# Splitting the next weights ahead of the normed input in the output products of a two-layer decoder step

## The chip, the cores and the metric

The kernel runs on one core of a Trainium2 chip. The metric is the device time of one execution, in microseconds (us). TensorE multiplies, VectorE and ScalarE work on tiles, GpSimd adds up squares, and SyncE issues the loads of the weights; each runs its own list of instructions in order, and they meet at semaphores. In the rows of the profile they are called PE (with PEld for its weight loads), DVE, ACT, POOL and SP.

## The reference

The reference is one inference step of a small decoder: 512 new prompt tokens and 8 sequences of 8 sample tokens, 576 tokens in all, of 1024 features. There are two layers. Each adds to the residual x a half SwiGLU, a mixer (gated delta rule in the first layer, stick-breaking attention in the second), another half SwiGLU, and a gated per-layer embedding. A projection that several of these end with has this form:

```python
x = x + 0.5 * _swiglu(_rms_norm(x, w['ffn1_norm'][i]), w['ffn1_w_in'][i], w['ffn1_w_out'][i])
h = _rms_norm(x, w['mix_norm'][i])
...
def _rms_norm(x, g):
    xf = x.astype(jnp.float32)
    y = xf * lax.rsqrt(jnp.mean(xf * xf, axis=-1, keepdims=True) + EPS)
    return (y * g.astype(jnp.float32)).astype(x.dtype)

def _swiglu(h, w_in, w_out):
    gu = h @ w_in
    gate, up = gu[..., :D_FF], gu[..., D_FF:]
    return (jax.nn.silu(gate) * up) @ w_out
```

All matrices are float32, D_FF is 2816.

## The kernel before

**Layout and arithmetic.** Activations lie transposed: features on the 128 partitions, 576 tokens in the free dimension. A product is computed tile by tile, each tile being 128 output features by 576 tokens. float32 values are kept as a high and a low part in TensorE's faster float32 format: for each block of 128 input features the function `multiply` (line 529) issues three matmuls, high by high, high by low and low by high, for each of two parts of the tokens. The parts are `PARTS = ((0, C0), (C0, T))` with `C0 = 288` and `T = 576`, so 288 columns each (lines 55 and 222). A tile with k blocks is thus 6k matmuls of 288 columns.

**Units and buffers.** Two tiles, m = 0 and m = 1, make a unit. The weights of a unit are loaded as one slot of `raw`, of which there are two. The split parts `w_hi` and `w_lo` have one place for m = 0 and one for m = 1. ScalarE makes `w_hi` with `split_hi` (line 478) as a rounded copy; it waits until the load has landed and until TensorE has finished the tile that last used that place. VectorE makes `w_lo` with `split_lo` (line 495) as the difference of `raw` and `w_hi`. So while TensorE works on one tile, the weights of the tile after it are split. SyncE loads a unit (`load_unit`, line 510) once `w_lo` of the unit two before it has been made.

**Output products.** A step of kind `upd` adds a product to the residual `xT`: four units, eight tiles, in the plan at lines 361 to 421. There are fourteen: three for each of the four SwiGLUs, over 8, 8 and 6 blocks of the hidden features (`GROUPS`, line 76), and one behind each mixer, over 8 blocks. Only the last of the three (6 blocks) and the two behind the mixers make the input of what follows. They carry `after` and `sums`: for each finished tile VectorE updates `xT` (line 3076), ScalarE makes `hx_hi`, the rounded x times gain, and `sqb`, the square (`act_renorm`, lines 2544 to 2554), VectorE makes `hx_lo` (`dve_renorm`, line 2564), and GpSimd adds the square to `ssum` (line 2581). The normalising factor is applied later, to the results of the next product: at that product's first tile TensorE sums `ssum` over the partitions (line 603) ahead of the last block, ScalarE takes the root into `std` (line 610), and VectorE the reciprocal into `rs` (line 614).

**What sets the order.** Everything is written out by hand. `in_pairs` (line 452) runs a body for each unit and tells it which tile's weights to split (`split`): those of the next unit of the step, and behind the last unit those of the first unit of the next step. In the six `upd` steps that carry `after`, the engines' bodies (lines 2929 to 2934 and 3071 to 3078) run, for each tile, first what the finished tile needs and then the split. In the other kinds of step, the `gu` step of the SwiGLU's input product for one, ScalarE splits first.

Of the kernel before, what the change touches and what calls it, by code (L numbers as in the profile page):

```python
# [48 lines left out]
def program(nc, A, O):  # L49
# [33 lines left out]
    with ctx:  # L83
# [160 lines left out]
        def halves(ap):  # L244
            return ap.rearrange("p (c n) -> p c n", c=2)

        def seqs(ap, n=TD):

            return ap.rearrange("p (b t) -> p b t", t=n)
# [85 lines left out]
        def pin_view(par, m):  # L335
            return praw[:, par].rearrange("p (k n) -> p k n", n=2 * P)[:, :, m * P:(m + 1) * P]
# [135 lines left out]
        def unit_no(s, i, r):  # L472
            return i * 2 + (s.n["unit"] + r)

        def slot_of(s, r):
            return raw[:, (s.n["unit"] + r) % 2, :], raw_in[(s.n["unit"] + r) % 2]

        def split_hi(act, target, m):

            s, i, r = target  # L480
            if s is None:
                return
            slot, landed = slot_of(s, r)
            k = (s.ka, s.kb)[m]
            act.wait_ge(landed, i * 32 + 32 * ((s.n["unit"] + r) // 2 + 1))
            if not (isinstance(i, int) and unit_no(s, i, r) == 0):
                act.wait_ge(tile_done, unit_no(s, i, r) * 2 + (m - 1))
            nc.scalar.activation(w_hi[:, m, 0:k], s.view(m, slot), ACT.Copy).then_inc(w_hi_done, 1)  # L488
            if s.kind == "ple":
                n = KD * s.n["ple"] + 2 * r  # L490
                if not (isinstance(i, int) and n + 4 * i + m < 2):
                    act.wait_ge(pin_done, i * 4 + (n + m - 1))
                nc.scalar.activation(pw_hi[:, m], pin_view((s.n["unit"] + r) % 2, m), ACT.Copy).then_inc(pw_hi_done, 1)
# [2047 lines left out]
        def x_rows_of(i):  # L2541
            return P if i < PT else TS

        def act_renorm(act, s, j, m):

            if s.after is not None:
                hi, hi_done = (hid_hi, hid_hi_done) if s.into is HID else (hx_hi, hx_hi_done)
                nc.scalar.activation(hi[:, ds(j, 1)], xT[:, ds(j, 1)], ACT.Copy,  # L2548
                                     scale=gain[:, ds(j + s.after, 1)]).then_inc(hi_done, 1)
            if s.sums:  # L2550
                q = KD * s.n["sum"]
                if not (isinstance(j, int) and q + j < 2):
                    act.wait_ge(ssum_done, j + (q - 1))
                nc.scalar.activation(sqb[:, m:m + 1], xT[:, ds(j, 1)], ACT.Square).then_inc(sq_done, 1)  # L2554

        def dve_renorm(dve, s, j):

            if s.after is not None:
                hi, lo = s.into or HX
                if s.into is HID:  # L2560
                    dve.wait_ge(hid_hi_done, j + (s.n["hid"] + 1))
                else:
                    dve.wait_ge(hx_hi_done, j + (KD * s.n["hx"] + 1))
                nc.vector.scalar_tensor_tensor(lo[:, ds(j, 1)], xT[:, ds(j, 1)], gain[:, ds(j + s.after, 1)],  # L2564
                                               hi[:, ds(j, 1)].bitcast(F32), ALU.mult, ALU.subtract
                                               ).then_inc(hid_done if s.into is HID else hx_done, 1)
# [330 lines left out]
        def _(act):  # L2897
# [6 lines left out]
            for s in plan:  # L2904
                def body(i, r, split):
                    N = unit_no(s, i, r)
                    u = i * 2 + r
                    first = isinstance(u, int) and u == 0 and s.stats and s.n["stat"]
                    if first:
                        act_stats(act, s.n["stat"])  # L2910
                    if s.kind == "gu":
                        split_hi(act, split, 0)
                        act.wait_ge(evac[0], N + 1)
                        if not (isinstance(u, int) and s.n["gu"] + u == 0):
                            act.wait_ge(hid_mul, u + s.n["gu"])
                        nc.scalar.activation(gate_f[:], gate_s[:], ACT.Silu).then_inc(silu_done, 1)
                        split_hi(act, split, 1)
                        act.wait_ge(hid_mul, u + (s.n["gu"] + 1))
                        nc.scalar.activation(hid_hi[:, ds(u, 1)], hid_f[:], ACT.Copy).then_inc(hid_hi_done, 1)  # L2919
                        move_rows(act, s, 1, fills_at(s, u, 1))  # L2920
                    elif s.kind == "lin":
                        if s.after is not None and u == 0:
                            act.wait_ge(tile_done, 2 * s.n["unit"])
                        for m in range(2):
                            if s.after is not None:
                                act_renorm(act, s, u * 2 + m, m)
                            split_hi(act, split, m)
                            move_rows(act, s, 1, fills_at(s, u, m))
                    elif s.kind == "upd":
                        for m in range(2):  # L2930
                            if s.after is not None or s.sums:
                                act.wait_ge(evac[m], N + 1 - m * (s.n["unit"] - s.n["eb"]))
                                act_renorm(act, s, u * 2 + m, m)
                            split_hi(act, split, m)
                    elif s.kind == "qkv":
                        for m in range(2):
                            c = u * 2 + m
                            split_hi(act, split, m)
                            act.wait_ge(evac[m], N + 1)
                            nc.scalar.activation(cv[:, m, 0:XC], xpad[:, m, 0:XC], ACT.Copy,  # L2940
                                                 scale=conv_w[:, 0, ds(c, 1)]).then_inc(tap_done, 1)
                            act.wait_ge(conv_step, c * CP + CP)
                            out = qkv[:, ds(c, 1)].squeeze(1)
                            nc.scalar.activation(out[:, 0:TP], cv[:, m, 0:TP], ACT.Silu).then_inc(conv_done, 1)
                            nc.scalar.activation(seqs(out[:, TP:T]), seqs(cv[:, m, CP + TP:], CP + TD)[:, :, 0:TD], ACT.Silu).then_inc(conv_done, 1)
                    elif s.kind == "ab":
                        ab_act(act, s, N, split)
                    elif s.kind == "gate":
                        for m in range(2 - s.alone):
                            gate_act(act, s, N, u, m, split)  # L2950
                    elif s.kind == "ple":
                        for m in range(2):
                            if s.end and (u, m) in ((2, 1), (3, 0)):
                                y_left(act, 2 * (2 * u + m - 5) + 1)
                            split_hi(act, split, m)
                            act.wait_ge(evac[m], N + 1 - m * (s.n["unit"] - s.n["eb"]))
                            buf = (gate_s, up_s)[m]
                            nc.scalar.activation(buf[:], buf[:], ACT.Sigmoid).then_inc(silu_done, 1)
                            act.wait_ge(x_add, u * 2 + (KD * s.n["ple"] + m + 1))
                            act_renorm(act, s, u * 2 + m, m)  # L2960
                            if s.end:
                                j = u * 2 + m
                                nc.scalar.activation(yT[:, j], xT[:, j], ACT.Copy, scale=gain[:, FIN + j:FIN + j + 1]).then_inc(y_done, 1)
                    else:
                        split_hi(act, split, 0)
                        split_hi(act, split, 1)
# [70 lines left out]
        def _(dve):  # L3037
# [4 lines left out]
            for s in plan:  # L3042
                def body(i, r, split):
                    N = unit_no(s, i, r)
                    u = i * 2 + r
# [25 lines left out]
                    elif s.kind == "upd":  # L3071
                        for m in range(2):
                            j = u * 2 + m
                            dve.wait_ge(tile_done, (tile_a, tile_b)[m])
                            x = xT[:, ds(j, 1)].squeeze(1)
                            nc.vector.scalar_tensor_tensor(halves(x), TOKENS[m], s.coef, halves(x), ALU.mult, ALU.add).then_inc(evac[m], 1)  # L3076
                            dve_renorm(dve, s, j)
                            split_lo(dve, split, m)
                    elif s.kind == "qkv":
                        for m in range(2):  # L3080
                            c = u * 2 + m
# [247 lines left out]
```

## Time and profile before

| what | value |
|---|---|
| median of 3 runs (lowest to highest) | 2609.31 us (2607.67 to 2610.5) |
| profiled execution, own time | 2611.66 us |
| its span | 2609.5 us |
| PE busy | 2547.4 us, 98% of the span |
| DVE, ACT, POOL busy | 51%, 35%, 10% |
| loads | 86 GB/s over the span |

The page of the profile gives each engine's busy time, the chain of work that ended last, and groups of instructions. The timeline lists instructions by start time with their durations and, in brackets, how long the engine had been idle before and what released it. Matmuls are pipelined: a matmul of 288 columns is shown with 0.29 us, but the next one starts some 0.12 us later, so TensorE's pace is read from start to start.

### The profile page before, as it was taken

Reading aid. Unit: us, or ns where it says so; the run is one execution under the profiler, and the core shown is the slowest. Engines: PE = TensorE matmul, PEld = TensorE weight load, DVE = VectorE, ACT = ScalarE, POOL = GpSimd, SP = SyncE. Lnnn points to the kernel's source line nnn. Section 1 sums busy time; section 2 is a strip of 40 time slices with the busy share of each in tenths; the row PEclk is TensorE's granted clock in tenths of the full one; section 3 lists DMA queues with packets and bytes.
Section 4 is the critical chain, followed back from the end, with each engine's and each line's share of the span. In section 5 each row is a group of like instructions: output and inputs, shape, how many; then the busy total and the mean of one; then the engine's idle time right before and its main releaser. Section 6 shows DMA issues by size and latency. Waiting matters only on the chain.

```text
span 2609.5 us, 52241 instructions
## 1 busy us (share of the span) xinstructions
PE 2547.4 (98%) x21981; PEld 2454.2 (94%) x21981; DVE 1325.9 (51%) x1739; ACT 916.6 (35%) x1384; POOL 270.4 (10%) x348
## 2 busy tenths in 40 slices
PE   8999999999999999999999999999999999999998
PEld 7999999998888999999999999999986699999998
DVE  4434347765555554343565443434557754344454
ACT  4222224454323432222343232222348832222244
POOL 2000002001223200000120000000133210000011
PEclk9999999999999899999999999999999999999999
DMA  5233322321011332332222442323303423232321
GB/s 149 81 87 90 93 72 93 97 81 32 20 36 52 99 97 88 89 96 81 85 93 81 126 135 81 96 81 89 116 14 106 146 81 90 88 93 85 93 97 57
DMA packets 308138, 225.96 MB, mean 87 GB/s; under 512 B 8270, under 2 KB 301567, under 8 KB 307967
## 3 DMA queue, kind: packets, MB, share of 16 engines
q1 hardware_dynamic: 307280, 224.26, 28.5%
q8 instruction: 82, 1.34, 0.2%
q14 instruction: 38, 0.31, 0.0%
q0 software_dynamic: 576, 0.00, 0.0%
q10 hardware_dynamic: 162, 0.04, 0.0%
HBM read 212.14 MB, written 12.13 MB: 86 GB/s over the span
## 4 chain that ended last, share of the span: by engine, by line
PE 92%; DVE 4%; ACT 2%; issue 1%; DMA 0%; POOL 0%; SPq 0%; DVEq 0%; POOLq 0%; ACTq 0%
PE ps L551 77%; DVE w_lo L503 1%; PE ps L2425 1%; PE ps L2459 1%; PE ps L570 1%; PE ps L1824 1%; PE ps L2467 1%; PE ps L1828 1%; PE ps L2364 1%; PE ps L1572 0%; ACT w_hi L488 0%; DVE xT L3076 0%; PE ps L2609 0%; PE ps L1835 0%; ACT sqb L2554 0%
## 5 line engine op out<-in xcount | busy, mean ns | idle before, releaser
L551 PE MATMUL ps<-hx_hi,w_hi 128*128 128x288 f32 x3730 | 1071.0, 287 | 4.0 <-DVE w_lo L503 3.2
L551 PE MATMUL ps<-hx_lo,w_hi 128*128 128x288 f32 x3730 | 1066.8, 286 | 0.0
L551 PE MATMUL ps<-hx_hi,w_lo 128*128 128x288 f32 x3730 | 1066.8, 286 | 0.0
L488 ACT ACTIVATE w_hi<-raw 128x1024 fp32r<-128x1024 f32 (+1 forms) x362 | 373.9, 1033 | 1095.7 <-PE ps L551 1095.3
L551 PEld LDWEIGHTS ps<-hx_hi,w_hi 128*128 128x128 f32 x3730 | 704.9, 189 | 8.0 <-DVE w_lo L503 4.0
L551 PEld LDWEIGHTS ps<-hx_lo,w_hi 128*128 128x128 f32 x3730 | 705.0, 189 | 0.3
L551 PEld LDWEIGHTS ps<-hx_hi,w_lo 128*128 128x128 f32 x3730 | 705.0, 189 | 0.0
L551 PE MATMUL ps<-hid_hi,w_hi 128*128 128x288 f32 x1920 | 554.0, 289 | 5.6 <-DVE w_lo L503 4.8
L551 PE MATMUL ps<-hid_hi,w_lo 128*128 128x288 f32 x1920 | 551.1, 287 | 0.0
L551 PE MATMUL ps<-hid_lo,w_hi 128*128 128x288 f32 x1920 | 551.0, 287 | 0.0
L503 DVE TENSOR_TENSOR w_lo<-raw,w_hi 128x1024 fp32r<-128x1024 f32 (+1 forms) x362 | 460.4, 1272 | 124.0 <-ACT w_hi L488 123.9
L551 PEld LDWEIGHTS ps<-hid_hi,w_hi 128*128 128x128 f32 x1920 | 364.6, 190 | 9.1 <-issue 8.6
L551 PEld LDWEIGHTS ps<-hid_hi,w_lo 128*128 128x128 f32 x1920 | 364.7, 190 | 0.1
L551 PEld LDWEIGHTS ps<-hid_lo,w_hi 128*128 128x128 f32 x1920 | 364.6, 190 | 0.0
L2581 POOL TENSOR_TENSOR ssum<-ssum,sqb 128x576 f32<-128x576 f32 x64 | 92.4, 1443 | 1808.1 <-issue 1216.5
L3060 DVE TENSOR_TENSOR up_s<-ps,rs 128x576 f32<-128x576 f32 x88 | 66.6, 757 | 308.0 <-PE ps L551 307.8
L3076 DVE SCALAR_TENSOR_TENSOR xT<-ps,xT 128x576 f32<-128x576 f32 x112 | 84.6, 755 | 249.8 <-PE ps L551 249.8
L3057 DVE TENSOR_TENSOR gate_s<-ps,rs 128x576 f32<-128x576 f32 x88 | 66.6, 757 | 215.4 <-PE ps L551 215.1
L2548 ACT ACTIVATE hx_hi<-xT,gain 128x576 fp32r<-128x576 f32 x56 | 43.3, 774 | 147.8 <-DVE xT L3076 147.8
L2919 ACT ACTIVATE hid_hi<-hid_f 128x576 f32 (+1 forms) x88 | 60.2, 685 | 54.9 <-DVE hid_f L3065 54.9
L2564 DVE SCALAR_TENSOR_TENSOR hx_lo<-xT,gain,hx_hi 128x576 fp32r<-128x576 f32 x64 | 51.9, 816 | 40.5 <-ACT hx_hi L2548 40.5
L3065 DVE TENSOR_TENSOR hid_f<-gate_f,up_s 128x576 f32<-128x576 f32 x88 | 66.7, 758 | 10.7 <-DVE up_s L3060 9.3
(477 smaller groups left out, 2277.9 us busy)
## 6 DMA issues: line engine op xcount, KB each, us to landing
raw<-in_ffn_w_in SPq DMA_DIRECT2D x176, 512.0 KB, 4.9
raw<-in_ffn_w_out SPq DMA_DIRECT2D x64, 512.0 KB, 4.0
raw<-in_a_w_in SPq DMA_DIRECT2D x33, 512.0 KB, 4.3
raw<-in_ffn_w_out SPq DMA_DIRECT2D x32, 384.0 KB, 3.4
raw<-in_ple_w_gate SPq DMA_DIRECT2D x8, 1024.0 KB, 5.2
raw<-in_w_kv SPq DMA_DIRECT2D x16, 512.0 KB, 4.1
k_page<-in_cache_k SPq DMA_DIRECT2D x16, 512.0 KB, 3.5
v_page<-in_cache_v SPq DMA_DIRECT2D x14, 512.0 KB, 4.8
```

The costliest lines, as they stand in the source:

```text
L488: nc.scalar.activation(w_hi[:, m, 0:k], s.view(m, slot), ACT.Copy).then_inc(w_hi_done, 1)
L503: nc.vector.tensor_tensor(w_lo[:, m, 0:k], s.view(m, slot), w_hi[:, m, 0:k].bitcast(F32), ALU.subtract).then_inc(w_lo_done, 1)
L551: last = nc.tensor.matmul(TILE[m][:, c0:c1], w[:, m, k], columns(h, k, c0, c1), start=k == 0 and a == 0, stop=k == k_all - 1 and a == 2)
L570: last = nc.tensor.matmul(PIN[:, c0:c1], w[:, m, k], columns(h, k, c0, c1), start=k == 0 and a == 0, stop=k == PK - 1 and a == 2)
L2548: nc.scalar.activation(hi[:, ds(j, 1)], xT[:, ds(j, 1)], ACT.Copy, scale=gain[:, ds(j + s.after, 1)]).then_inc(hi_done, 1)
L2564: nc.vector.scalar_tensor_tensor(lo[:, ds(j, 1)], xT[:, ds(j, 1)], gain[:, ds(j + s.after, 1)], hi[:, ds(j, 1)].bitcast(F32), ALU.mult, AL ...
L2581: nc.gpsimd.tensor_tensor(ssum[:], ssum[:], sqb[:, m], ALU.add).then_inc(ssum_done, 1)
L2919: nc.scalar.activation(hid_hi[:, ds(u, 1)], hid_f[:], ACT.Copy).then_inc(hid_hi_done, 1)
L3057: nc.vector.tensor_tensor(halves(gate_s[:]), TOKENS[0], halves(rs[:]), ALU.mult).then_inc(evac[0], 1)
L3060: nc.vector.tensor_tensor(halves(up_s[:]), TOKENS[1], halves(rs[:]), ALU.mult).then_inc(evac[1], 1)
L3065: nc.vector.tensor_tensor(hid_f[:], gate_f[:], up_s[:], ALU.mult).then_inc(hid_mul, 1)
L3076: nc.vector.scalar_tensor_tensor(halves(x), TOKENS[m], s.coef, halves(x), ALU.mult, ALU.add).then_inc(evac[m], 1)
```

## The change

A small test `at_end` is added, true for the last tile of a step. In `upd` steps the split of the next weights moves ahead, for each tile but the last: on ScalarE ahead of the wait for VectorE's update of `xT`, of `hx_hi` and of `sqb`; on VectorE to between the update of `xT` and `hx_lo`. For the last tile the order stays. The change's title also names equal parts of 288 columns; these are in the kernel before already and no line of the diff touches them.

```diff
+        def at_end(s, u, m):
+            return isinstance(u, int) and 2 * u + m == 2 * s.units - 1
+
...
                     elif s.kind == "upd":
                         for m in range(2):
+                            if not at_end(s, u, m):
+                                split_hi(act, split, m)
                             if s.after is not None or s.sums:
                                 act.wait_ge(evac[m], N + 1 - m * (s.n["unit"] - s.n["eb"]))
                                 act_renorm(act, s, u * 2 + m, m)
-                            split_hi(act, split, m)
+                            if at_end(s, u, m):
+                                split_hi(act, split, m)
...
                             nc.vector.scalar_tensor_tensor(halves(x), TOKENS[m], s.coef, halves(x), ALU.mult, ALU.add).then_inc(evac[m], 1)
+                            if not at_end(s, u, m):
+                                split_lo(dve, split, m)
                             dve_renorm(dve, s, j)
-                            split_lo(dve, split, m)
+                            if at_end(s, u, m):
+                                split_lo(dve, split, m)
```

The order of ScalarE's instructions at the end of the first SwiGLU's last output product, from its seventh tile on, before. `w_hi` of 128x1024 is a weight tile of the next step:

```order
L2548 ACTIVATE hx_hi<-xT,gain 128x576
L2554 ACTIVATE sqb<-xT 128x576
L488 ACTIVATE w_hi<-raw 128x1024
L2548 ACTIVATE hx_hi<-xT,gain 128x576
L2554 ACTIVATE sqb<-xT 128x576
L488 ACTIVATE w_hi<-raw 128x1024
L610 ACT_TABLE_LOAD
```

The same place with the change (the line numbers are three higher):

```order
L488 ACTIVATE w_hi<-raw 128x1024
L2551 ACTIVATE hx_hi<-xT,gain 128x576
L2557 ACTIVATE sqb<-xT 128x576
L2551 ACTIVATE hx_hi<-xT,gain 128x576
L2557 ACTIVATE sqb<-xT 128x576
L488 ACTIVATE w_hi<-raw 128x1024
L610 ACT_TABLE_LOAD
```

The seventh tile's split has moved ahead of its `hx_hi` and `sqb`; the last tile's stands where it stood.

VectorE at the same place, from the seventh tile's update of `xT` to the reciprocal, before:

```order
L3076 SCALAR_TENSOR_TENSOR xT<-ps,xT 128x576
L2564 SCALAR_TENSOR_TENSOR hx_lo<-xT,gain,hx_hi 128x576
L503 TENSOR_TENSOR w_lo<-raw,w_hi 128x1024
L3076 SCALAR_TENSOR_TENSOR xT<-ps,xT 128x576
L2564 SCALAR_TENSOR_TENSOR hx_lo<-xT,gain,hx_hi 128x576
L503 TENSOR_TENSOR w_lo<-raw,w_hi 128x1024
L614 RECIPROCAL rs<-std 128x576
```

And with the change:

```order
L3082 SCALAR_TENSOR_TENSOR xT<-ps,xT 128x576
L503 TENSOR_TENSOR w_lo<-raw,w_hi 128x1024
L2567 SCALAR_TENSOR_TENSOR hx_lo<-xT,gain,hx_hi 128x576
L3082 SCALAR_TENSOR_TENSOR xT<-ps,xT 128x576
L2567 SCALAR_TENSOR_TENSOR hx_lo<-xT,gain,hx_hi 128x576
L503 TENSOR_TENSOR w_lo<-raw,w_hi 128x1024
L614 RECIPROCAL rs<-std 128x576
```

`w_lo` and `hx_lo` have changed places for the seventh tile, as for the six before it, and not for the last. The lists of TensorE, GpSimd and SyncE are the same in both programs.

## Rows read from the trace of the kernel before

**Rows 1.** Page, part 1: busy us, share of the span, instructions.
```profile
PE 2547.4 (98%) x21981; PEld 2454.2 (94%) x21981; DVE 1325.9 (51%) x1739; ACT 916.6 (35%) x1384; POOL 270.4 (10%) x348
```

**Rows 2.** Waits of PE: waiting line, releaser, us in total, times, longest.
```profile
PE ps L551 <- DVE w_lo L503: 8.1, 21, 0.7
```

**Rows 3.** Chain that ended last: start us, us, what, of an undisturbed stretch.
```profile
932.33 345.70 PE ps L551 x2820
```

**Rows 4.** Timeline of PE, first, second and fourth SwiGLU's last output product: start us, us.
```profile
377.71 0.29 PE L551 MATMUL ps<-hid_hi,w_hi 128*128 128x288 f32 x1
...
401.02 0.29 PE L551 MATMUL ps<-hid_hi,w_hi 128*128 128x288 f32 x1
...
405.31 0.29 PE L551 MATMUL ps<-hid_lo,w_hi 128*128 128x288 f32 x1
...
405.97 0.36 PE L551 MATMUL ps<-hid_hi,w_hi 128*128 128x288 f32 x1 [0.38 <-DVE w_lo L503]
...
415.49 0.39 PE L551 MATMUL ps<-hx_hi,w_hi 128*128 128x288 f32 x1 [0.46 <-DVE w_lo L503]
...
1273.44 0.29 PE L551 MATMUL ps<-hid_hi,w_hi 128*128 128x288 f32 x1
...
1311.26 0.39 PE L551 MATMUL ps<-hx_hi,w_hi 128*128 128x288 f32 x1 [0.47 <-DVE w_lo L503]
...
2494.23 0.29 PE L551 MATMUL ps<-hid_hi,w_hi 128*128 128x288 f32 x1
...
2532.05 0.39 PE L551 MATMUL ps<-hx_hi,w_hi 128*128 128x288 f32 x1 [0.48 <-DVE w_lo L503]
```

**Rows 5.** Timeline of all engines around one tile, the first of the third unit.
```profile
401.22 0.76 DVE L3076 SCALAR_TENSOR_TENSOR xT<-ps,xT 128x576 f32<-128x576 f32 x1 [0.51 <-PE ps L551]
...
402.01 0.78 ACT L2548 ACTIVATE hx_hi<-xT,gain 128x576 fp32r<-128x576 f32 x1 [2.94 <-DVE xT L3076]
...
402.69 0.67 ACT L2554 ACTIVATE sqb<-xT 128x576 f32<-128x576 f32 x1
...
402.82 0.82 DVE L2564 SCALAR_TENSOR_TENSOR hx_lo<-xT,gain,hx_hi 128x576 fp32r<-128x576 f32 x1 [0.84 <-ACT hx_hi L2548]
...
403.27 0.83 ACT L488 ACTIVATE w_hi<-raw 128x768 fp32r<-128x768 f32 x1
...
403.44 1.48 POOL L2581 TENSOR_TENSOR ssum<-ssum,sqb 128x576 f32<-128x576 f32 x1 [3.55 <-ACT sqb L2554]
...
404.13 1.60 DVE L503 TENSOR_TENSOR w_lo<-raw,w_hi 128x768 fp32r<-128x768 f32 x1 [0.49 <-ACT w_hi L488]
```

**Rows 6.** Timeline of all engines, a tile of the input product before.
```profile
372.03 0.76 DVE L3057 TENSOR_TENSOR gate_s<-ps,rs 128x576 f32<-128x576 f32 x1 [2.53 <-PE ps L551]
...
372.09 0.84 ACT L488 ACTIVATE w_hi<-raw 128x768 fp32r<-128x768 f32 x1 [3.67 <-PE ps L551]
...
372.97 0.96 DVE L503 TENSOR_TENSOR w_lo<-raw,w_hi 128x768 fp32r<-128x768 f32 x1 [0.18 <-ACT w_hi L488]
```

**Rows 7.** Timelines of DVE, POOL and PE, last tile and start of the next product.
```profile
415.36 0.74 DVE L3076 SCALAR_TENSOR_TENSOR xT<-ps,xT 128x576 f32<-128x576 f32 x1
...
418.47 1.66 DVE L503 TENSOR_TENSOR w_lo<-raw,w_hi 128x1024 fp32r<-128x1024 f32 x1 [0.70 <-ACT w_hi L488]
...
417.56 1.48 POOL L2581 TENSOR_TENSOR ssum<-ssum,sqb 128x576 f32<-128x576 f32 x1 [3.21 <-ACT sqb L2554]
...
420.74 1.13 PE L603 MATMUL ps<-ssum,ones 128*128 128x288 f32 x4
```

**Rows 8.** Timeline of SP: issues of the third and fourth unit's weights.
```profile
380.36 11.84 SPq L516 DMA_DIRECT2D raw<-in_ffn_w_out  x4
```

**Rows 9.** Page, part 6: DMA issues, KB each, median us to landing.
```profile
raw<-in_ffn_w_out SPq DMA_DIRECT2D x32, 384.0 KB, 3.4
```

**Rows 10.** Timeline of DVE, one tile of the product behind the first mixer.
```profile
907.70 0.76 DVE L3076 SCALAR_TENSOR_TENSOR xT<-ps,xT 128x576 f32<-128x576 f32 x1 [1.08 <-PE ps L551]
...
910.83 1.66 DVE L503 TENSOR_TENSOR w_lo<-raw,w_hi 128x1024 fp32r<-128x1024 f32 x1 [0.70 <-ACT w_hi L488]
```

## The prediction

> **What bounds the kernel now.** I read the page first. TensorE is busy for 98% of the span [rows 1], and nearly all of the chain that ended last is its own matmuls, so a change of order on ScalarE and VectorE can only act where TensorE stands still for them. The table of TensorE's waits, read next, has one row on the split weights: 8.1 us in 21 waits, the longest 0.7 us [rows 2]. To see where these are I went through TensorE's timeline. Sixteen of the 21 lie in four places, four in each: the last output product (6 blocks) of each SwiGLU, at the start of its second, third and fourth unit and at the start of the product behind it. The rows show the third and fourth wait of the first place, at 405.97 and 415.49, and the last one of the second and of the fourth place [rows 4]. The two products behind the mixers have none in their inside.
>
> An idle time in brackets counts from a modelled end, so I measure the loss from start to start. Undisturbed, 2820 matmuls take 345.70 us [rows 3], 0.1226 us each. A unit here is 72 matmuls, 8.83 us; from 405.97 to 415.49 it took 9.52 us. At 405.97 the pieces are seen: the last matmul of the tile before started at 405.31, the next could have followed at 405.43 and came 0.54 us later, and a first matmul behind a wait takes a little under 0.1 us more. For the whole product, the four starts run from 377.71 to 415.49, 37.78 us; 37.82 us in the second and in the fourth place [rows 4]; the third, which repeats the pattern, has 37.80 us. Together 151.22 us. Without waits, 4 x 288 matmuls at 0.1226 us are 141.23 us. **The loss is 9.99 us.**
>
> Why TensorE waits there is read around one tile [rows 5]. TensorE starts the next tile at 401.02 [rows 4]; VectorE begins the update of x at 401.22, which I call E. ScalarE waits for the update, makes hx_hi and sqb, and starts w_hi only at 403.27, E+2.05. VectorE's w_lo starts at 404.13 and ends at 405.73, E+4.51. The tile that TensorE has meanwhile is worth 36 x 0.1226 = 4.41 us from 401.02, so it would need the weights at 405.43, E+4.21. They are late by 0.3 us, plus about 0.24 us from w_lo's end to the first matmul. After such a late start the next weights, counted from a delayed tile, come in time; hence one wait for each two tiles.
>
> **The change, part by part.** Nothing is added or removed. On ScalarE, w_hi (0.83 us) goes ahead of the wait for the update and of hx_hi (0.78) and sqb (0.67). It then needs only TensorE's tile and the landed load. The input product just before has this order, and there w_hi starts 0.06 us behind the evacuation, and w_lo 0.94 us behind it, to last 0.96 us [rows 6]. I take this as it stands for the new order: w_hi from E+0.06 to E+0.90, w_lo from E+0.94 to E+1.90. It is needed at E+4.21, so 2.3 us of slack takes the place of 0.3 us of lateness. For the weights of the next step, of 8 blocks, w_lo without company takes 1.22 us and w_hi 1.04, so E+2.36: still 1.85 us of slack. Both bounds of the gain follow: all of the loss, 9.99 us, if nothing else is late; nothing, if w_hi waits for something else. The rows of the input product are the nearest, so I take the upper end: **-10.0 us**.
>
> What is moved back: hx_hi would start at about E+0.8 (as before), sqb end at E+2.2 instead of E+2.14, and hx_lo run from about E+1.8 to E+2.6 instead of E+1.60 to E+2.42. These matter only at the next product, whose blocks are used in turn, 6 matmuls or 0.74 us each. The seventh tile's is used some 9 us after its tile ended, so 0.2 us are hidden. The last tile keeps its order. GpSimd's add starts at about E+2.3 instead of E+2.22 and must be done before the next one, 4.4 us later: hidden too.
>
> Loads: SyncE's waits hang on w_lo of every second tile, which now comes some 2.6 us earlier, so loads start earlier and none starts later. The other side is that w_hi now asks for its load up to 2 us earlier. The third unit's was issued at 380.36 [rows 8]; two pieces of 3.4 us one behind the other [rows 9] have landed by 387.2, while the tile after which it is asked for ends near 391.8. Slack 4.6 us: cost 0.
>
> Products behind the mixers: there w_lo ends at 912.49, 4.79 us behind E = 907.70 [rows 10], and a tile of 48 matmuls lasts 5.88 us. Nothing waits, so the new order is worth nothing there, 0. The other eight output products carry no input for what follows and are the same program on ScalarE, and on VectorE too. The equal parts of 288 columns are in both programs: 0.
>
> One thing more stands in these rows. w_lo of 128x768 takes 0.96 us where GpSimd rests [rows 6] and 1.60 us behind the add that runs from 403.44 to 404.92 [rows 5]; it ends 0.81 us behind the add's end. That is nearly all of its own time, as if it had stood still until then. Without these 0.64 us the weights would have been there at E+3.87 and TensorE would not have waited. In the new order w_lo is over before the add begins at E+2.3. The Trainium skill, "SBUF — State Buffer", section "Who interferes with whom", says that a VectorE instruction with two SBUF inputs contends with a GpSimd instruction that reads SBUF and that whichever came first holds the pair for its whole length. By that rule the trace agrees in both its numbers, and hx_lo, which would now come first, holds the add back by some 0.4 us, to end near E+4.1; by a mere sharing both would be a little longer. By the one the sum is 10.0 us and by the other too, but under the rule the company moves to hx_lo and the add and cannot follow w_lo.
>
> **What is late next.** At the start of the next product TensorE needs the sum of squares ahead of the last block. Now the last tile's update starts at 415.36, the add ends at 419.04, 3.68 us later, and TensorE comes to it at 420.74 [rows 7]. With the wait gone the product starts 0.20 us ahead of E, and 42 matmuls on, at E+4.95, it wants the sum; the add ends at E+3.68. So 1.3 us of slack remain, where there were 1.7. The second tile's weights are at 420.13, E+4.77 [rows 7]; they are needed after a whole tile and the sum's matmuls, about E+6.5. Neither turns into a wait.
>
> **The sum.** Profiled execution: 2611.66 - 9.99 = 2601.7 us, its span 2609.5 - 9.99 = 2599.5 us. That execution stands 2.35 us above the median of the runs, so for the median 2609.31 - 9.99 = **2599.3 us**, 0.38% faster. The three runs lie 2.8 us apart, and I call differences under 0.2%, 5.2 us, no change: from 2604.1 to 2614.5 us.
>
> **The rivals.** (A) The forecast. All sixteen waits go. Chance 0.84.
>
> (B) The twelve waits inside go, but the four ahead of the following product come back at its start, since that start hangs on the last tile's chain (update, sqb, add) and not on TensorE. Price: each is worth 9.52 - 8.83 = 0.69 us, so 2.8 us are given back: 2602.1 us. For it: the chain is unchanged for the last tile, and the slack shrinks. Against: 1.3 us are left. Chance 0.07.
>
> (C) The change does not do what it says: w_hi goes ahead in the list but waits, for the load or for TensorE's end of tile. All waits stay: 2609.3 us; half of them: 2604.3 us. For it: the new wait is for two semaphores, one of them the load. Against: the slack of 4.6 us and the input product, where just this order works. Chance 0.06, a third of it for half.
>
> (D) Slower. The sum of squares becomes the bound: split and lock together push sqb and the add of the last two tiles back until TensorE stands at the sum's matmuls at the six products that follow. It decides from 1.3 us of extra delay on. To lose 5.2 us against before it would have to eat 10 us of gain as well, 15.2 / 6 = 2.5 us each, so 3.8 us of delay. One w_hi and one w_lo with the add's stop are 0.83 + 1.60 = 2.4 us, and the last tile's order has neither ahead of it. Price at a full 4.4 us of delay (one tile): 6 x 3.1 = 18.6, less 10: 2618 us. Chance 0.03.
>
> **How the numbers follow.** Faster by over 0.2%: A, B and a little of C, 0.92. Within: the rest of C, 0.05. Slower: D, 0.03. The range takes A with the scatter of medians of about 2.5 us to either side, and on the upper side B and its scatter: 2596.8 to 2603.6 us. Half of C, C and D lie outside.
>
> **What would show it.** The waits of TensorE on w_lo fall from 21 to about 5 and from 8.1 us to about 1; each of the four products takes 35.3 us from its first matmul to that of the next; w_lo of 128x768 has about 0.96 us everywhere and starts 0.9 us behind the update of x; hx_lo or the add is the one that grows. The first matmul of the sum at the next product starts 5.15 us behind the product's first. I am wrong if waits on w_lo stay (C), if one on ssum or hx_lo appears at the next product (B, D), or if the stretch shrinks and a later one grows.

## The result and the profile after

The changed kernel takes 2596.69 us (median of 6 runs, 2592.87 to 2599.85), beside 2610.2 us of the kernel before (6 runs, 2607.67 to 2611.51). The ratio is 0.995, with a 95% interval from 0.9938 to 0.9962: 13 us faster, between 10 and 16. The forecast was 2599.3 us, 10.0 us faster, and the median lies 0.1 us below the low end of the range. The profiled execution took 2598.09 us, its span is 2596.0 us.

In TensorE's table of waits the row that it was all about has shrunk; what [rows 2] had as 8.1 us in 21 waits is now (total, times, longest):

```profile
PE ps L551 <- DVE w_lo L503: 2.5, 6, 1.5
```

All sixteen of the four places are gone. Of the 2.5 us left, 1.5 are a single wait at 18.5, right behind the kernel's start, which took 0.7 us before; the other five are 0.2 to 0.3 us each.

In the timeline of PE, the first of the four places. The columns are start and duration, in us:

```profile
377.64 0.29 PE L551 MATMUL ps<-hid_hi,w_hi 128*128 128x288 f32 x1
...
412.79 0.29 PE L551 MATMUL ps<-hid_lo,w_hi 128*128 128x288 f32 x1
...
412.92 0.29 PE L551 MATMUL ps<-hx_hi,w_hi 128*128 128x288 f32 x1
...
418.06 1.13 PE L603 MATMUL ps<-ssum,ones 128*128 128x288 f32 x4
```

From the output product's first matmul at 377.64 to that of the next product at 412.92 are 35.28 us, where [rows 4] had 37.78 (377.71 to 415.49). The last matmul before stands 0.13 us ahead of it: no wait is left. The chain that ended last says the same of a longer stretch. Before, it was broken at the second place's four waits; now TensorE's matmuls are in one piece from the second unit of the first product behind the first mixer to the start of the gated embedding, and in another, as long, behind the second mixer:

```profile
927.70 381.70 PE ps L551 x3114
...
2142.22 381.70 PE ps L551 x3114
```

381.70 / 3114 is 0.1226 us for each, the undisturbed pace of [rows 3], though both stretches now hold a whole output product of the kind that waited.

One tile of the third unit, on all engines, answers to [rows 5]:

```profile
399.89 0.76 DVE L3082 SCALAR_TENSOR_TENSOR xT<-ps,xT 128x576 f32<-128x576 f32 x1 [1.78 <-PE ps L551]
...
399.95 0.84 ACT L488 ACTIVATE w_hi<-raw 128x768 fp32r<-128x768 f32 x1 [2.33 <-PE ps L551]
...
400.82 0.96 DVE L503 TENSOR_TENSOR w_lo<-raw,w_hi 128x768 fp32r<-128x768 f32 x1 [0.18 <-ACT w_hi L488]
...
401.70 0.81 DVE L2567 SCALAR_TENSOR_TENSOR hx_lo<-xT,gain,hx_hi 128x576 fp32r<-128x576 f32 x1
...
402.11 1.68 POOL L2584 TENSOR_TENSOR ssum<-ssum,sqb 128x576 f32<-128x576 f32 x1 [2.73 <-ACT sqb L2557]
```

With E = 399.89, w_hi starts at E+0.06 and w_lo runs from E+0.93 to E+1.89, against E+0.94 to E+1.90 in the forecast. w_lo takes 0.96 instead of 1.60 us, and the add 1.68 instead of 1.48: it is the add now that has company, from hx_lo.

**Where the time came from.** Marks that are in both traces, after minus before: TensorE's first matmul of the second unit behind the first place, which has a short wait in both, starts at 426.11 for 428.79, -2.68 us. First before, then after:

```profile
428.79 0.36 PE L551 MATMUL ps<-hx_hi,w_hi 128*128 128x288 f32 x1 [0.30 <-DVE w_lo L503]
```

```profile
426.11 0.36 PE L551 MATMUL ps<-hx_hi,w_hi 128*128 128x288 f32 x1 [0.30 <-DVE w_lo L503]
```

Of this, -0.07 stood at 377 already, so 2.61 us at this place. The same difference over the second, third and fourth place is 2.64, 2.63 and 2.64 us, 10.5 us together. The rest of the 13.5 us between the spans is 0.07 us at the start, 2.0 us from the first mixer to the second unit of the product behind it, and 1.0 us in the attention, and no wait on w_lo went there. What that is had to be found out.

### The profile page after: what moved, and what is told of

It is laid out like the page before. It is cut to its first block, busy times and chain, and to the rows that moved or that the text cites. A ratio compares the mean times of both kernels' runs of the same rounds, so it can differ in the third digit from the quotient of the medians.

```text
span 2596.0 us, 52241 instructions
## 1 busy us (share of the span) xinstructions
PE 2540.4 (98%) x21981; PEld 2450.5 (94%) x21981; DVE 1300.3 (50%) x1739; ACT 916.7 (35%) x1384; POOL 283.3 (11%) x348
## 4 chain that ended last, share of the span: by engine, by line
PE 95%; DVE 3%; ACT 1%; issue 1%; DMA 0%; POOL 0%; SPq 0%; DVEq 0%; POOLq 0%; ACTq 0%
PE ps L551 80%; PE ps L2425 1%; PE ps L570 1%; PE ps L2459 1%; PE ps L1824 1%; PE ps L1828 1%; PE ps L2467 1%; PE ps L2364 1%; PE ps L1572 0%; PE ps L2612 0%; PE ps L1835 0%; PE ps L1674 0%; PE ps L2461 0%; PE ps L2462 0%; PE ps L1659 0%
## 5 line engine op out<-in xcount | busy, mean ns | idle before, releaser
L503 DVE TENSOR_TENSOR w_lo<-raw,w_hi 128x1024 fp32r<-128x1024 f32 (+1 forms) x362 | 436.9, 1207 | 111.0 <-ACT w_hi L488 110.8
L2584 POOL TENSOR_TENSOR ssum<-ssum,sqb 128x576 f32<-128x576 f32 x64 | 105.3, 1645 | 1784.5 <-issue 1215.6
L3071 DVE TENSOR_TENSOR hid_f<-gate_f,up_s 128x576 f32<-128x576 f32 x88 | 66.7, 758 | 10.7 <-DVE up_s L3066 9.3
L3074 DVE TENSOR_TENSOR hid_lo<-hid_f,hid_hi 128x576 f32 (+1 forms) x88 | 66.2, 752 | 0.4 <-issue 0.4
L3104 DVE SCALAR_TENSOR_TENSOR cv<-xpad,conv_w,cv 128x600 f32<-128x600 f32 x72 | 60.6, 842 | 5.2 <-DVE cv L3104 0.2
```

Of the source, the lines that this page charges most:

```text
L503: nc.vector.tensor_tensor(w_lo[:, m, 0:k], s.view(m, slot), w_hi[:, m, 0:k].bitcast(F32), ALU.subtract).then_inc(w_lo_done, 1)
L2584: nc.gpsimd.tensor_tensor(ssum[:], ssum[:], sqb[:, m], ALU.add).then_inc(ssum_done, 1)
L3071: nc.vector.tensor_tensor(hid_f[:], gate_f[:], up_s[:], ALU.mult).then_inc(hid_mul, 1)
L3074: nc.vector.tensor_tensor(hid_lo[:, ds(u, 1)], hid_f[:].unsqueeze(1), hid_hi[:, ds(u, 1)].bitcast(F32), ALU.subtract).then_inc(hid_done, 1)
L3104: nc.vector.scalar_tensor_tensor(cv[:, m, 0:XC], xpad[:, m, j:j + XC], conv_w[:, j, ds(c, 1)], cv[:, m, 0:XC], ALU.mult, ALU.add).then_inc ...
```

## The experiments

Seven kernels were timed, each beside the kernel before on the same chip; the ratios are to its runs there.

**Theories.** 1: w_lo was late because GpSimd's add of the squares stood in its way; the order matters only since it takes w_lo out from under the add. 2: the chain update, hx_hi, sqb, w_hi, hx_lo, w_lo was too long in itself. 3: the 3 us beyond the four places are scatter of the mixers' stretch. 4: they come from the reorder behind the mixers.

### ScalarE's part alone

```diff
                             if not at_end(s, u, m):
                                 split_hi(act, split, m)
...
-                            if not at_end(s, u, m):
-                                split_lo(dve, split, m)
                             dve_renorm(dve, s, j)
-                            if at_end(s, u, m):
-                                split_lo(dve, split, m)
+                            split_lo(dve, split, m)
```

> Only ScalarE's part of the change: w_hi ahead of hx_hi and sqb, VectorE keeps hx_lo ahead of w_lo. E is the start of a tile's update of x. Theory 1 (w_lo was late because it stood behind GpSimd's add, which holds the input path the two share): w_hi is ready at E+0.9, hx_lo runs E+1.6 to E+2.4, the add is in line from E+2.3, gets its turn first and runs to about E+3.9, and w_lo ends at about E+4.7. The waits on w_lo stay, about 21, and the time is that of before, 2610 us within 3. Theory 2 (only the length of the chain ahead of w_lo counts): w_lo runs from E+2.4 to E+3.3 and takes 0.96 us, the sixteen waits are gone, time 2597 to 2600 us.

Measured: 2608.91 us (11 runs), ratio 0.9997 (0.9988 to 1.0007). Nothing gained. TensorE's waits on w_lo are 22, 9.4 us. The timeline, for DVE and then POOL:

```profile
401.14 0.76 DVE L3082 SCALAR_TENSOR_TENSOR xT<-ps,xT 128x576 f32<-128x576 f32 x1 [0.51 <-PE ps L551]
402.74 0.82 DVE L2567 SCALAR_TENSOR_TENSOR hx_lo<-xT,gain,hx_hi 128x576 fp32r<-128x576 f32 x1 [0.84 <-ACT hx_hi L2551]
403.48 2.17 DVE L503 TENSOR_TENSOR w_lo<-raw,w_hi 128x768 fp32r<-128x768 f32 x1
...
403.36 1.47 POOL L2584 TENSOR_TENSOR ssum<-ssum,sqb 128x576 f32<-128x576 f32 x1 [3.55 <-ACT sqb L2557]
```

w_lo was started 0.6 us earlier in its tile than before (E+2.34 for E+2.91) and ended at E+4.51, to the hundredth where it ended before: 0.82 us behind the add's end, against 0.81 before. It takes 2.17 us now. Its end hangs on the add, not on its own start. This is what theory 1 says and not what theory 2 says.

### VectorE's part alone

```diff
-                            if not at_end(s, u, m):
-                                split_hi(act, split, m)
                             if s.after is not None or s.sums:
...
-                            if at_end(s, u, m):
-                                split_hi(act, split, m)
+                            split_hi(act, split, m)
```

> Only VectorE's part: w_lo ahead of hx_lo, while ScalarE makes w_hi last, as before. w_lo still starts at E+2.9, behind w_hi, under the add, and ends at E+4.5; now hx_lo (0.82 us) stands behind it and holds VectorE to E+5.3, past the end of the next tile at E+4.4. Theory 1 and 2 alike: VectorE becomes the bound in the four SwiGLU output products, 5.25 us a tile where before two tiles took 9.44, so 0.5 us for each of 7 tiles in 4 places, 13 to 17 us slower than before: 2620 to 2628 us. If instead the order on VectorE is what brought the gain by itself: 2600 us.

Measured: 2622.83 us (5 runs), ratio 1.0034 (1.0021 to 1.0047): slower by 9 us (5 to 12). The median lies inside the expected 2620 to 2628 us, but the loss is smaller than the expected 13 to 17. The trace says the same: the four products take 39.99, 40.20, 40.18 and 40.20 us from their first matmul to that of the next, 9.4 us more than before. 33 waits on w_lo, 14.6 us in all. DVE's timeline has every tile in the same grip:

```profile
399.79 1.55 DVE L503 TENSOR_TENSOR w_lo<-raw,w_hi 128x768 fp32r<-128x768 f32 x1 [2.15 <-ACT w_hi L488]
401.26 0.81 DVE L2567 SCALAR_TENSOR_TENSOR hx_lo<-xT,gain,hx_hi 128x576 fp32r<-128x576 f32 x1
401.99 0.75 DVE L3079 SCALAR_TENSOR_TENSOR xT<-ps,xT 128x576 f32<-128x576 f32 x1
...
404.88 1.54 DVE L503 TENSOR_TENSOR w_lo<-raw,w_hi 128x768 fp32r<-128x768 f32 x1 [2.15 <-ACT w_hi L488]
```

hx_lo stands behind a late w_lo and holds up the next tile's update. The add (404.19 to 405.60 in this round) lies over w_lo again. The round is 5.09 us (404.88 - 399.79), not the 5.25 that I had, against 4.72 for a tile before. So half of the change, put in by itself, costs nearly what the whole one brings. VectorE's order is right only once w_hi comes early.

### The old order with a later add

```diff
             pool.wait_ge(sq_done, j + (q + 1))
+            if s.kind == "upd" and not (isinstance(j, int) and j == KD - 1):
+                pool.wait_ge(w_lo_done, j + (2 * s.n["unit"] + 3))
```

(GpSimd's loop over the units is written out in the `upd` steps, so that the last tile can be told apart.)

> The old order on both engines, but GpSimd's add of the squares waits, in the output products and for all tiles but the last, until w_lo of that tile's turn is made. Theory 1: w_lo of 128x768 falls from 1.60 to 0.96 us and ends at E+3.9 instead of E+4.5, before TensorE wants it at E+4.2; the sixteen waits are gone without any reordering, and the time is as with the change, 2597 to 2601 us. Theory 2 (the chain is too long in itself): the waits stay, 2610 us.

Measured: 2598.29 us (6 runs), ratio 0.9949 (0.9935 to 0.9964), not to be told from the whole change. The order on ScalarE and VectorE is the old one; 5 waits on w_lo remain, 1.6 us. DVE and POOL:

```profile
399.33 0.76 DVE L3082 SCALAR_TENSOR_TENSOR xT<-ps,xT 128x576 f32<-128x576 f32 x1 [0.55 <-PE ps L551]
400.93 0.82 DVE L2564 SCALAR_TENSOR_TENSOR hx_lo<-xT,gain,hx_hi 128x576 fp32r<-128x576 f32 x1 [0.85 <-ACT hx_hi L2548]
402.24 0.96 DVE L503 TENSOR_TENSOR w_lo<-raw,w_hi 128x768 fp32r<-128x768 f32 x1 [0.49 <-ACT w_hi L488]
...
403.33 1.41 POOL L2583 TENSOR_TENSOR ssum<-ssum,sqb 128x576 f32<-128x576 f32 x1 [3.00 <-DVE w_lo L503]
```

w_lo starts at E+2.91 as before and ends at E+3.87, the figure of the prediction. Holding the add back until w_lo is through takes away the twelve waits inside the products. At the start of the next product a little is left. There w_lo is the longer one of 128x1024, and the update of its tile started at 408.15:

```profile
411.27 1.23 DVE L503 TENSOR_TENSOR w_lo<-raw,w_hi 128x1024 fp32r<-128x1024 f32 x1 [0.70 <-ACT w_hi L488]
...
412.23 0.29 PE L551 MATMUL ps<-hid_lo,w_hi 128*128 128x288 f32 x1
412.55 0.39 PE L551 MATMUL ps<-hx_hi,w_hi 128*128 128x288 f32 x1
```

It ends at E+4.35, and the next product's first matmul starts 0.32 us behind the last of this one, where the changed kernel has 0.13. The four products take 35.47 us each instead of 35.28, and the start of the next one costs another 0.1 us as before; by the two traces the later add brings 9.3 of the 10.5 us. So theory 1 is the cause of nearly all of it, and theory 2 keeps a small part: for the longer w_lo the old chain is 0.2 us too long even with nothing in its way.

### The new order only behind the mixers

```diff
         def at_end(s, u, m):
-            return isinstance(u, int) and 2 * u + m == 2 * s.units - 1
+            return isinstance(u, int) and 2 * u + m == 2 * s.units - 1 or s.ka != KD
```

> The new order only in the two output products behind the mixers (8 blocks), the old one behind the SwiGLUs. The change gained some 13 us, of which 10.5 stand at the four SwiGLU places in the two traces; about 2 us lie in and just behind the first mixer, 1 in the second. Theory 3 (those 3 us are the clock and the mixers' own scatter): 2610 us within 2, waits as before. Theory 4 (the reorder behind the mixers brings them): 2607 us, and the first product behind the first mixer shorter by about 0.6 us.

Measured: 2610.2 us (11 runs), ratio 0.9997 (0.9988 to 1.0005). Theory 4 falls; the reorder is worth nothing there. The 0.6 us in the product behind the first mixer is not the order's either: the last 366 matmuls of that output product take 47.1 us before and 46.5 after the change, but 47.6 with the order only here and 46.5 with ScalarE's part alone. The profiled execution, at 2617.05 us, is the longest of its eleven, and shows where the scatter lies.

### The new order only behind the SwiGLUs

The same line with `s.ka == KD` in place of `s.ka != KD`.

> The new order only in the four output products of the SwiGLUs (6 blocks), the old one behind the mixers. Theory 3 (the 10.5 us at the four places are the change, the rest of its 13 us was scatter of the mixers' stretch): 2597 to 2601 us, as with the whole change. Theory 4 (the reorder behind the mixers gives 2 to 3 us): 2600 to 2603 us, and always above the whole change.

Measured: 2599.05 us (5 runs), ratio 0.9958 (0.9945 to 0.9972), as theory 3 has it. The interval of the whole change overlaps this one, so these two kernels alone would not tell theory 3 from theory 4; the kernel with the order behind the mixers only does.

The scatter shows in the chain of work that ended last, between two groups of 54 matmuls: one in the last product ahead of the first mixer, one in the product that follows the mixer's output product. Columns: start us, us. With the order only behind the mixers:

```profile
617.27 6.62 PE ps L551 x54
...
931.36 6.62 PE ps L551 x54
```

Only behind the SwiGLUs:

```profile
615.18 6.62 PE ps L551 x54
...
917.74 6.62 PE ps L551 x54
```

That is 314.09 and 302.56 us; between the same groups the kernel before has 307.63 and the changed one 305.69. The two are 11.5 us apart, more than the 10.5 us of the four places, over the same instructions. The view by windows gives TensorE's granted clock over this stretch (the number behind the five busy times), as a share of its full 2.4 GHz; it is a mean over time at that level and at 1.2 GHz. First the order only behind the mixers, then only behind the SwiGLUs:

```profile
617.30:931.40 314.10, 296.61 (x3649) 264.61 (x3649) 172.83 (x331) 108.66 (x275) 88.22 (x84) 0.91 0.18 51
```

```profile
615.20:917.70 302.50, 284.46 (x3649) 252.46 (x3649) 176.08 (x331) 108.56 (x274) 85.53 (x84) 0.95 0.18 53
```

0.91 and 0.95, with 0.93 before and 0.94 after the change. A lower granted clock goes with a longer mixer. As an estimate from these rows: with only two levels, a mean of 0.91 over 314.1 us is some 57 us at 1.2 GHz, and 0.95 over 302.5 us some 30. At half the clock the 26 us between can cost 13 us at most, and 11.5 were seen. It does not go with the order: ScalarE's part alone has 305.1 us at 0.94 and VectorE's part alone 312.7 us at 0.91.

Each timed run also lists its mean granted clock over the whole kernel, and that allows a comparison at equal clock. The runs of the kernel before are the 36 of these experiments. Against them stand 22 runs of the four kernels that have lost the waits: the change itself, the later add, the order only behind the SwiGLUs, and the next one. At 0.990, where both have most runs, twelve before come to 2609.32 us on average, and six (two of each kernel but the last) to 2598.72: 10.6 us. At the other readings, some with a single run, the difference is 9.0 to 10.9 us. A straight line in the clock through all 58 runs, with one step for the lost waits, puts the step at **10.1 us** (9.6 to 10.7). That fits what the traces of the places say, 10.5 us, and 9.3 for the later add. Clock and time go together in both groups, from 2614.5 us at 0.987 to 2605.6 at 0.991 before, and from 2605.5 to 2596.6 after. The six runs of the changed kernel had a mean clock of 0.9907, the 36 of the kernel before 0.9891.

### The new order for the last tile too

`at_end` returns `False`.

> The new order for the last tile of each output product too. Slack as worked out: w_hi (1.04) goes ahead of the last hx_hi and sqb, w_lo (1.22) ahead of hx_lo, so the last add runs behind hx_lo and ends at about E+4.6 instead of E+3.7, and TensorE asks for the sum of squares at E+4.95. Theory of the slack: still no wait, time as with the change within 1 us, 2596 to 2600 us. Rival D (the sum of squares becomes the bound): a wait on ssum at the six products that follow, 0.3 to 0.5 us each, 2599 to 2602 us.

Measured: 2597.03 us (5 runs), ratio 0.9948 (0.9934 to 0.9961), no wait on the sum. The last tile and the sum's matmuls, from the timelines of DVE, POOL and PE:

```profile
412.71 0.76 DVE L3082 SCALAR_TENSOR_TENSOR xT<-ps,xT 128x576 f32<-128x576 f32 x1 [1.31 <-PE ps L551]
...
415.14 1.94 POOL L2584 TENSOR_TENSOR ssum<-ssum,sqb 128x576 f32<-128x576 f32 x1 [2.47 <-ACT sqb L2557]
...
417.65 1.13 PE L603 MATMUL ps<-ssum,ones 128*128 128x288 f32 x4
```

The add ends at E+4.37, the sum is taken at E+4.94: 0.6 us of slack are left. The exception for the last tile is worth nothing measurable here; it keeps 0.7 us more in hand.

### Past the slack

The kernel with the later add, with the last tile's add waiting too:

```diff
-            if s.kind == "upd" and not (isinstance(j, int) and j == KD - 1):
+            if s.kind == "upd":
```

> As the old order with late adds, but the last tile's add waits for its w_lo too. Its w_lo of 128x1024 is made at about E+4.3, the add then takes 1.4 us and ends at about E+5.8, while TensorE asks for the sum at E+4.95. If the slack is as worked out, TensorE waits on ssum at each of the six products that follow, 0.8 to 1.1 us each, 5 to 7 us in all: 2603 to 2606 us instead of 2598. If the start of the next product does not hang on the last add: 2598 us, no such wait.

Measured: 2605.28 us (9 runs), ratio 0.9982 (0.9972 to 0.9993), inside what was expected. POOL and PE:

```profile
417.53 1.40 POOL L2583 TENSOR_TENSOR ssum<-ssum,sqb 128x576 f32<-128x576 f32 x1 [3.00 <-DVE w_lo L503]
...
419.03 1.21 PE L603 MATMUL ps<-ssum,ones 128*128 128x288 f32 x4 [0.58 <-issue]
```

The add ends at 418.93, E+5.88 with E = 413.05, and TensorE goes on 0.1 us later; unhindered it would have been there at E+4.95. The table of waits puts this under "issue", not under the add:

```profile
PE ps L603 <- issue: 4.8, 7, 0.9
```

One of the seven, 0.3 us at the sum of a later product, is in every kernel. The price is better read from start to start: from the next product's first matmul to its second unit, the first three of the six products take 6.82, 7.01 and 9.48 us instead of the 6.00, 5.90 and 8.42 of the later add, and all six together 6.0 us more. The medians give 7.0 us (2605.28 - 2598.29), but they come from two chips. So rival D is a real mechanism with a place and a price, 6 to 7 us over the six products, and more than half of the gain was given back. It needs a delay past 1.3 us, and the change has none.

## Why the prediction was right, and where it was off

**What bounds, and the loss.** Right. The sixteen waits in four places were the whole matter, and all sixteen went. The forecast of about 1 us for what stays was short: 2.5 us, of which 1.5 at the kernel's start. The loss was reckoned as 9.99 us and the four places gave 10.5. Most of the missing 0.14 us for each place lies behind the point where I stopped the clock: from the next product's first matmul to the sum's matmuls there were 5.25 us [rows 4, 7] and are now 5.14 (418.06 - 412.92). A start behind a wait is slow in its first matmul, and I had counted that for three of four starts.

**The cost of the parts.** Right to a few hundredths for the split: w_hi at E+0.06, w_lo done at E+1.9, slack of 2.3 us. Taking the rows of the input product for the new order was the step that made it easy. The seven other tiles' hx_lo and adds stayed hidden, and no wait for a load appeared. The add was foretold to end near E+4.1 and ended at E+3.90 (402.11 + 1.68 - 399.89).

**Why w_lo was late.** The remark about the lengthened w_lo turned out to be the cause and not a side matter. By the Trainium skill, "SBUF — State Buffer", section "Who interferes with whom", whichever comes first holds the shared pair for its length. The runs agree: the add ended 1.27 to 1.28 us behind hx_lo's end whether it had started 0.2 us ahead of that end (before, and ScalarE's part alone), 0.4 us (after) or 0.67 us (the last tile in the new order), and w_lo ended 0.8 us behind the add's end whether it started 0.8 or 1.35 us ahead of it. A mere sharing would have the end move with the start. What comes behind the other's end is 0.13 to 0.15 us short of the instruction's own 1.41 or 0.96 us. In the prediction this stood as a remark at the end; it forecast the sum from the length of the chain, which by itself would also have let ScalarE's part alone pass as the whole change.

**The median.** The predicted 2599.3 us, against 2596.69, and a gain of 10.0 us against 13.5 between the medians. The kernel before came out 0.9 us above the median that the forecast started from (2610.2 for 2609.31), which hides a part of the miss. In the two traces, 0.5 us are the loss that was mis-sized. 2.0 us lie in the first mixer and behind it, where TensorE's granted clock was 0.94 for 0.93; the range had to cover this and did not. I took the scatter from three runs 2.8 us apart, and the kernel before alone later spread from 2605 to 2615.5 us over 23 runs. It could have been asked of the view by windows, which shows a clock of 0.93 in that stretch before the change, where the first SwiGLU has 1.00. The 1.0 us in the attention is not explained: the mean clock there is 0.98 in both traces, and in the six of the nine profiled executions with that clock the stretch took 174.2 to 175.4 us whatever the order. Why six runs of the changed kernel had more of the high clock stays open too; the kernel with the order only behind the SwiGLUs did not, at a mean of 0.9894. The 3 us by which the medians differ beyond the waits lie in stretches that the other runs show moving without the order: chance, and no merit or fault of the mechanism.

**The rivals.** B (waits come back at the next product) did not happen: 1.3 us of slack held, and the forced case shows what it would have cost. C (does not do what it says) did not happen as a whole, but each half of the change alone is just that: it gains nothing. D did not happen either.

## What to carry to other kernels

When an instruction takes longer in one place than in another with the same shape, look at what ran beside it before reordering: here its end hung on a GpSimd instruction's end, and either moving it out of the way or holding that other instruction back gave 9 to 10.5 us, while making it start earlier without leaving the add's shadow gave nothing. A reorder over two in-order engines must be judged as one: half of it lost 9 us. And a gain should be compared at equal granted clock where each run lists it; it brought a 13 us difference back to the 10 us that the waits explain.

## What the runs showed of the hardware

- A VectorE tensor_tensor with both inputs in SBUF (128x768) takes 0.96 us alone, 1.60 us when it starts 0.8 us ahead of the end of a GpSimd add of two SBUF tiles, and 2.17 us when it starts 1.35 us ahead of it. In both cases it ends 0.8 us behind the add.
- VectorE's update of x, which reads PSUM and one SBUF input, kept its 0.74 to 0.76 us in all these kernels, also where the add ran beside it. In the later add it started at 399.33 beside an add from 398.92 to 400.33, which took its 1.41 us as well.
- The add of the squares (128x576) takes 1.41 us where no hx_lo or w_lo is ahead of it, and 1.68 and 1.94 us when it starts 0.4 and 0.67 us ahead of hx_lo's end; each time it ends 1.27 to 1.28 us behind that end.
- The stretch of the first mixer, with the same instructions, took from 302.5 to 314.1 us in the nine profiled executions, with a mean granted clock of 0.95 and 0.91 at the two ends. Over whole runs the clock of 0.987 to 0.991 goes with 2614.5 to 2605.6 us for the kernel before.
